# Placing the first group of modulation row products between the two halves of a chunk in a two-stream hybrid trunk

## The reference

```
m = SiLU(cond) @ mod_w + mod_b           # 1024 x 9216: nine vectors of 1024 for each stream
x += 1/2 * gate1 * SwiGLU_1(RMSNorm(x) * (1 + scale1) + shift1)
x += gate_m * W_out [A(h) | B(h) | C(h) | D(h)]      # attention, conv, DeltaNet, Fourier
x += 1/2 * gate2 * SwiGLU_2(RMSNorm(x) * (1 + scale2) + shift2)
SwiGLU(h) = (SiLU(h @ w1) * (h @ w3)) @ w2           # w1, w3: 1024 x 2816, w2: 2816 x 1024
```

## Time and profile before

| | us |
|---|---|
| median of 3 timed runs | 3383.18 |
| lowest and highest | 3373.24, 3384.57 |
| the profiled execution: its time | 3371.52 |
| the profiled execution: span on the core | 3369.8 |
| TensorE busy | 3081.8 (91% of the span) |
| VectorE, ScalarE, GpSimd busy | 1467.9, 803.2, 253.3 |
| mean granted clock of TensorE | 0.937 of full speed |

### The profile page before, as it was taken

The page is one execution under the profiler, slowest core; times in us unless marked ns, Lnnn a source line. Parts: engine busy times, 40 slices in busy tenths (PEclk is TensorE's granted clock), DMA queues, the critical chain, the costliest instruction groups (busy, mean ns, idle before and its releaser), DMA issues.

```text
span 3369.8 us, 58553 instructions
## 1 busy us (share of the span) xinstructions
PE 3081.8 (91%) x24855; PEld 2876.3 (85%) x24855; DVE 1467.9 (44%) x2406; ACT 803.2 (24%) x1155; POOL 253.3 (8%) x305
## 2 busy tenths in 40 slices
PE   5999999897779989999989999989876998999997
PEld 3999999894578788999989999989745888999997
DVE  3333444415355553343355444451433654544444
ACT  2222211322322232212223222222322223322221
POOL 2000000100022100000010000010001321000001
PEclk6999999997779999999999999999966899999998
DMA  6345322121000125434421222212200002122221
GB/s 237 102 161 170 131 76 84 51 63 38 0 4 4 39 69 169 163 130 142 149 75 38 75 75 75 75 63 76 72 4 2 4 3 76 38 75 75 75 75 44
DMA packets 163107, 258.95 MB, mean 77 GB/s; under 512 B 11868, under 2 KB 130884, under 8 KB 162592
## 3 DMA queue, kind: packets, MB, share of 16 engines
q1 hardware_dynamic: 140960, 174.57, 15.8%
q0 software_dynamic: 22016, 82.46, 7.3%
HBM read 253.85 MB, written 3.15 MB: 76 GB/s over the span
## 4 chain that ended last, share of the span: by engine, by line
PE 63%; issue 24%; DMA 5%; DVE 5%; ACT 1%; POOLq 1%; DVEq 1%; POOL 1%; ACTq 0%
PE ps L561 43%; PE ps L548 17%; DMA PT<-mod_w 4%; PE ps L584 1%; POOLq L438 1%; PE ps L808 1%; DMA ub<-mixer_tables 0%; DVE ast L1599 0%; DVE pexp L1608 0%; DVE PT L1365 0%; DVEq L1366 0%; POOL dB L524 0%; PE ps L852 0%; DVE cv L1566 0%; DVE PT L1645 0%
## 5 line engine op out<-in xcount | busy, mean ns | idle before, releaser
L561 PE MATMUL ps<-hh,uh 128*128 128x320 f32 x3744 | 864.3, 312 | 58.7 <-DVE hl L1392 48.6
L561 PE MATMUL ps<-hl,uh 128*128 128x320 f32 x3744 | 858.2, 311 | 0.0
L561 PE MATMUL ps<-hh,ul 128*128 128x320 f32 x3744 | 857.4, 310 | 0.0
L561 PEld LDWEIGHTS ps<-hh,uh 128*128 128x128 f32 x3744 | 629.6, 189 | 80.5 <-issue 69.1
L561 PEld LDWEIGHTS ps<-hl,uh 128*128 128x128 f32 x3744 | 631.0, 189 | 0.0
L561 PEld LDWEIGHTS ps<-hh,ul 128*128 128x128 f32 x3744 | 630.6, 189 | 0.0
L1357 DVE TENSOR_TENSOR ul<-raw,uh 128x1024 fp32r<-128x1024 f32 x322 | 390.6, 1235 | 270.9 <-ACT uh L1060 255.2
L1402 DVE SCALAR_TENSOR_TENSOR xT<-ps,modT,xT 128x128 f32<-128x128 f32 x736 | 371.5, 547 | 302.5 <-PE ps L561 301.3
L1060 ACT CAST uh<-raw 128x1024 fp32r<-128x1024 f32 x322 | 323.7, 1046 | 480.4 <-PE ps L561 420.9
L1422 DVE SCALAR_TENSOR_TENSOR PT<-ps,PT 128x640 f32<-128x640 f32 x88 | 72.5, 824 | 776.6 <-PE ps L561 776.6
L561 PE MATMUL ps<-gh,uh 128*128 (+1 forms) x1408 | 325.0, 312 | 15.2 <-DVE ul L1357 14.3
(11 more groups left out here) (241 smaller groups left out, 2507.8 us busy)
## 6 DMA issues: line engine op xcount, KB each, us to landing
raw<-ffn_w SPq DMA_DIRECT2D x264, 512.0 KB
PT<-mod_w POOLq DMA_DIRECT2D x72, 1024.0 KB, 6.2
raw<-w_in SPq DMA_DIRECT2D x40, 512.0 KB
raw<-w_out SPq DMA_DIRECT2D x8, 768.0 KB
ub<-mixer_tables POOLq DMA_DIRECT2D x2, 2176.0 KB, 8.3
out<-PT SPq DMA_DIRECT2D x5, 512.0 KB, 2.6
PT<-x_sample SPq DMA_DIRECT2D x4, 512.0 KB, 6.9
raw<-w_out SPq DMA_DIRECT2D x16, 128.0 KB
```

The costliest lines, as they stand in the source:

```text
L561: last = pe.matmul(pair(q)[:, lo:hi], wt[:, wk * P:(wk + 1) * P], mv(mk, lo, hi), start=start and i == 0 and p_ == 0, stop=stop and i == n ...
```

## The change

In TensorE's loop over blocks with modulation, the first row group, with its wait for `acc_used`, is given to `up(i, 0)` as its `between`: it is called behind the w1 product of chunk 0 and ahead of the w3 product. The second row group stays where it is, between the halves of chunk 1. Nothing changes on the other engines.

```diff
                     with pe.Fori(1, 1 + pairs) as i:
-                        up(i, 0)
                         n = i + (first - 1)
-                        pe.wait_ge(acc_used.sem, acc_used.at(l, abase + 8 * i - 8))
-                        modulation_rows(ml, 2 * n, 0)
-                        up(i, 1, lambda: modulation_rows(ml, 2 * n + 1, 1))
+
+                        def rows(half):
+                            if half == 0:
+                                pe.wait_ge(acc_used.sem, acc_used.at(l, abase + 8 * i - 8))
+                            modulation_rows(ml, 2 * n + half, half)
+                        up(i, 0, lambda: rows(0))
+                        up(i, 1, lambda: rows(1))
                         modulation_cols(ml, n)
                         down(i - 1, n)
```

## The result

| | before | after |
|---|---|---|
| median of 5 timed runs, us | 3378.14 | 3358.39 |
| lowest and highest | 3373.24, 3384.57 | 3357.19, 3359.34 |
| span of the profiled execution | 3369.8 | 3356.2 |

The changed kernel is faster by 19.75 us; the ratio is 0.994, with a 95% interval of 0.9924 to 0.9957. The forecast was a gain of 18 us and 3360 us, range 3351 to 3378.

A forecast was written before the change was run, and what follows sets the result against it. TensorE, busy 91% of the span, was taken as the bound, with 19.2 us lost waiting for modulation loads. Less 1.2 us kept back, the gain is 18 us: 3378.2 less 18 is 3360 us, range 3351 to 3378.

The forecast's parts named there:

- The price of the wait: Second row groups of 16 blocks take 52.81 us, first groups 33.63; the difference, 19.2 us, is waiting for modulation loads.
- The loads' landing: In an ordinary block the second load, issued at 216.0, lands before TensorE wants it at 230.4.
- bad-side bound: Loads get only what the weights leave: 5.26 MB at 343 GB/s, landing at 229.6 to 229.9; gain 13 us.
- good side: The second load still takes 7.97 us from issue, lands at 224, 6 us early; the whole 19.2 us goes.
- The 1.2 us kept back: Part of the 19.2 us assumed to stay, for the first blocks of the two feed-forwards; hence 18 us.
- the 6 us that the bad side kept: Wait left over: 1.8 us in three slow blocks, 3.1 in the two first blocks, a small part elsewhere.
- The rule of packets: DMA engines take turns between queues by packet; loads (3.8 KB against 1.3 KB) get most bandwidth, gaining 19.2 us.
- rival 2: Loads are served after the weights whenever issued, landing stays at 231: gain 0 to 3 us, 3377 us; chance 0.09.
- The moved wait costs nothing: TensorE's wait for the residuals, now before 213.4, is met by VectorE at 207.5, 5.9 us early.
- What is late next: ScalarE's weights land at about 230 and may land until 235.7 before column products wait: about 5.5 us spare.
- Rival 1: Second load lands within 1 us late in most blocks, 0.6 us left each: gain about 9, 3369 us; chance 0.16.
- Rival 3: Loads delay the weights, ScalarE's cast waits and column products wait: slower, 3417 us at 210 GB/s; chance 0.05.

The follow-up runs named there:

- experiment 1: Kernel before, with each mod_w transfer in the modulated blocks cut to one eighth (modulation wrong): 3362.6 us, ratio 0.9959.
- experiment 2: Changed kernel with mod_w transfers in the modulated blocks cut to one eighth (modulation wrong): 3364.5 us, ratio 0.9965 against the kernel before.
- experiment 4: The change in the 7 blocks of the first feed-forward only, the other 9 as before: 3366.1 us, ratio 0.997 against the kernel before.
- experiment 9: Changed kernel with the second row group half a product earlier, inside the w1 product of chunk 1: 3408.9 us, ratio 1.0093 against the kernel before.
- experiment 3: Kernel before with only the wait for the residuals moved ahead of the w3 product of chunk 0: 3377.4 us, ratio 1.0002.
- experiment 7: Changed kernel with the first row group one product earlier, ahead of chunk 0: 3377.1 us, ratio 0.9998 against the kernel before.
- experiment 5: Kernel before with the second row group moved behind the w3 product of chunk 1, the first left in place: 3400.4 us, ratio 1.0066.

## Why the prediction was right, point by point

- **The price of the wait, 19.2 us**: right. 19.07 us of it went in the profiled execution, 19.75 in the timed runs, and experiments 1, 2 and 4 show it to be the wait for the loads, spread over the blocks, and nothing else within them. (In time as a whole experiments 1 and 2 gained only 12 to 14 us, for the surplus outside the blocks.)
- **The loads' landing**: the bad-side bound was the true one. 5.26 MB at 343 GB/s gave a landing 0.5 us or more ahead of its use; it came 0.6 us ahead (225.3 for 225.9). My reason for leaning to the good side, that the load had 14.4 us and its own 7.97 us to compare, was wrong: it took 13.7. So the whole wait went, as on the good side, by a landing as late as on the bad one, and the 18 us was nearer than its reason. That much is luck: the bad-side sum had left half a microsecond of room, and with half a product less (experiment 9) the kernel is slower than before.
- **The 1.2 us kept back, and the 6 us that the bad side kept**: mis-sized, measured 0.07 to 0.1 us. The step that failed is that the slow blocks and the first blocks keep part of their loss. The first blocks have it easiest: there the second load lands 11.1 and 12.6 us after its issue, where the ordinary block took 13.7, and experiment 9 costs them 0.40 (125.46) and 1.50 us where the others lose 3.0 on average. The loads are issued at 114.40 there and the first weights at 114.00, so less is queued ahead of them; even so their first packet came only at 118.29, behind 0.97 MB of weights. The long tails of the three slow blocks did not return.
- **The rule of packets** from the Trainium skill ("DMA: Bandwidth & Descriptors", section "Queues, rings and completion order"): this case agrees, 418 packets against 453. But the early landing that I drew from it left out the time before the first packet, 4.35 us from the first issue, in which none of the loads' bytes moved. The other rule (section "Issuing engines are not separate DMA queues"), that an earlier issue from POOL brings no bandwidth, was as much of the truth: the pair landed in 10.9 and 13.7 us. Against rival 2 I held that the dip was there only because nothing was issued; the 1.58 us from an issue to its first packet are in it as well.
- **The moved wait costs nothing**: right, experiment 3 alone and experiment 7 for where it begins to cost, one product earlier, 1.3 us a block.
- **What is late next**: right in place, and nearly in size. ScalarE's cast was to begin near 230 in the old times, 225.5 in the new ones; it began at 226.31. The copy ended at 228.87 with the columns at 234.23; less the 0.7 us that the forecast took for the hand-over, 4.7 us to spare, forecast 5.5. Experiment 2 shows that this lateness costs TensorE nothing.
- **Rival 1** (only partly hidden): did not happen, though by 0.5 us; experiment 9 shows what it would have looked like. **Rival 2** (no effect): excluded by the windows. **Rival 3** (weights become the bound): no wait of L548 for L1088 in the blocks.
- **The sum**: 3378.2 for before was 3378.1; the 18 should have been 19.2, 1.6 us of error in all.

## What to carry to other kernels

Where a buffer is set free by one group of work and needed by the next, count the work that stands between the two and move one of the groups until it covers the load, on the side whose ends are not tight. The same 14.1 us of products between the groups cost nothing with the first group moved up; with the second moved back they brought a new wait of 1.2 us a block and a lower clock (experiment 5). One product further up than needed cost 1.3 us a block (experiment 7). Before issuing a load earlier, add up the bytes of both streams that have to pass and take the landing from the sum, not from the load's latency alone: here that gave 229.6 to 229.9 in the old times, 225.1 to 225.4 in the new ones, and 225.3 was measured. Such a small room has to be tried on both sides: half a product less cost 52 us (experiment 9). A gain can be priced before it is made from windows around the group that waits and the like group that does not.

## What the runs showed of the hardware that was not expected

- Waits of about the same length did not cost the same. In experiment 7 TensorE waited 1.3 us in each block ahead of the first group and the granted clock stayed at 1.00. In experiment 5 it waited 1.2 us in each block between the second row group and the column products, and the mean clock of both stretches was 0.97: 3.4 us at 1.2 in place of 2.4 GHz in 13 of the 16 blocks, 22 us on top of 20 us of waits. In the one the wait stands between weight products and the row products, in the other between the row products and the column products. Why the one falls and the other does not was not tried further.
- Two queues on the same DMA engines took turns one packet for one (418 and 453), so the queue with 4 KB packets got 79% of the bytes beside one with 1 KB packets; but a load issued into a full stream of weights waited 4.35 us for its first packet, while 1.6 MB of weights passed (4.35 to 4.9 us in the 14 ordinary blocks, 3.9 and 4.0 in the two first ones with 1.0 MB), against 1.6 us with idle engines. In the kernel before, in ordinary blocks, it was 1.6 us as well, though 0.2 to 0.4 MB of weights still passed in that time.
